# Rotary embedding and token-layout transposes inside the query/key/value projection, with its columns in the order value, key, query

## The reference

```python
q, k, v = jnp.split(xn @ w_qkv, 3, axis=-1)      # each (T, 1024): 8 heads x 2 maps x 64
q = rope(q, pos); k = rope(k, pos)               # x1*cos - x2*sin, x2*cos + x1*sin, halves of 64
# prompt: softmax over q k of both maps, a = p0 - lam * p1, o = a v; sample: the same over paged keys + new keys
return y, k, v                                   # rotated k rows and v rows are outputs too
```

## Time and profile before

| | us |
|---|---|
| median of three runs | 1459.0 |
| the profiled execution | 1462.04 |
| its span | 1460.7 |
| last scaling of the projection starts | 836.55 |
| first score matmul of the attention starts | 877.95 |

### The profile page before, as it was taken

One profiled execution on the slowest core, in us unless ns is written; L12 is line 12 of the kernel. 1 busy time (PEld: TensorE's weight loads), 2 busy tenths in 40 slices (PEclk: granted clock), 3 DMA queues, 4 the chain that ended last, 5 costly groups with the idle time before them and its releaser, 6 DMA issues.

```text
span 1460.7 us, 20977 instructions
## 1 busy us (share of the span) xinstructions
PE 1286.9 (88%) x8470; PEld 797.5 (55%) x8470; DVE 587.6 (40%) x1164; ACT 408.0 (28%) x717; POOL 146.9 (10%) x189
## 2 busy tenths in 40 slices
PE   6799999989879799999989959976987979999995
PEld 5676688866657543333347636654665755333332
DVE  3555367655333521212154574415533351221212
ACT  3443322254332211111153304434433221111112
POOL 5100031110002010101010060000000201110100
PEclk9899997799989799999999989978998979999998
DMA  8474354358638069999945737301873814999993
GB/s 239 143 211 125 114 161 124 100 174 288 236 126 340 22 257 421 420 421 421 422 155 158 241 101 259 117 1 58 291 248 129 337 41 191 421 422 420 421 421 118
DMA packets 112822, 340.16 MB, mean 233 GB/s; under 512 B 7486, under 2 KB 75402, under 8 KB 84048
## 3 DMA queue, kind: packets, MB, share of 16 engines
q1 hardware_dynamic: 107296, 322.20, 58.8%
q0 software_dynamic: 4992, 15.47, 3.4%
q10 hardware_dynamic: 432, 1.11, 0.2%
HBM read 328.21 MB, written 10.54 MB: 232 GB/s over the span
## 4 chain that ended last, share of the span: by engine, by line
PE 65%; DMA 17%; DVE 9%; issue 5%; ACT 3%; SPq 1%; POOL 1%; POOLq 0%; ACTq 0%; DVEq 0%
DMA arena<-in_w_exp_up 14%; PE ps L1961 10%; PE ps L547 8%; PE ps L549 8%; PE ps L548 8%; PE ps L2025 2%; PE ps L1440 2%; PE ps L1496 2%; PE ps L1415 2%; PE ps L2005 2%; PE ps L1480 2%; PE ps L1401 2%; DMA stg<-in_w_mem_k 1%; DVE wl L541 1%; PE ps L1428 1%
## 5 line engine op out<-in xcount | busy, mean ns | idle before, releaser
L1961 PE MATMUL ps<-arena,mkv 128*64 128x512 f32 x1024 | 230.0, 601 | 27.3 <-DMA arena<-in_w_exp_up 21.8
L547 PE MATMUL ps<-bx,wh 128*128 128x320 f16 (+1 forms) x640 | 194.5, 304 | 41.0 <-DVE bx L772 15.5
L548 PE MATMUL ps<-bx,wh 128*128 128x320 f16 (+1 forms) x640 | 194.3, 304 | 0.0
L549 PE MATMUL ps<-bx,wl 128*128 128x320 f16 (+1 forms) x640 | 194.1, 303 | 0.0
L541 DVE SCALAR_TENSOR_TENSOR wl<-stg,wh 128x1024 f16<-128x1024 f32 x128 | 157.8, 1272 | 87.4 <-ACT wh L534 86.5
L534 ACT ACTIVATE wh<-stg 128x1024 f16<-128x1024 f32 x128 | 128.4, 1049 | 216.8 <-PE ps L549 193.6
L1961 PEld LDWEIGHTS ps<-arena,mkv 128*64 128x64 f32 x1024 | 82.1, 138 | 170.7 <-issue 164.9
L2117 DVE TENSOR_TENSOR arena<-ps,arena 128x512 f16<-128x512 f32 x64 | 44.1, 688 | 143.2 <-ACT arena L2084 92.4
L547 PEld LDWEIGHTS ps<-bx,wh 128*128 128x128 f16 x640 | 65.0, 102 | 66.9 <-issue 34.7
L547 PE MATMUL ps<-arena,wh 128*128 128x320 f16 x288 | 88.4, 307 | 3.7 <-DVE arena L1363 3.0
L2121 DVE COPY arena<-ps 128x1 f32<-128x1 f32 x32 | 5.1, 158 | 211.6 <-PE ps L1983 211.6
(11 more groups left out here) (412 smaller groups left out, 1867.0 us busy)
## 6 DMA issues: line engine op xcount, KB each, us to landing
arena<-in_w_exp_gate SPq DMA_DIRECT2D x64, 1024.0 KB, 15.1
arena<-in_w_exp_up SPq DMA_DIRECT2D x64, 1024.0 KB, 17.2
arena<-in_w_exp_down SPq DMA_DIRECT2D x32, 1024.0 KB, 17.7
stg<-in_w_exp_down SPq DMA_DIRECT2D x32, 1024.0 KB, 17.5
arena<-in_cache_mem_k SPq DMA_DIRECT2D x16, 1024.0 KB, 6.9
arena<-in_cache_mem_v SPq DMA_DIRECT2D x16, 1024.0 KB, 5.2
stg<-in_w_in_a SPq DMA_DIRECT2D x28, 512.0 KB, 4.8
stg<-in_w_qkv_c SPq DMA_DIRECT2D x20, 512.0 KB, 4.6
```

Of the source, the lines that this page charges most:

```text
L547: nc.tensor.matmul(out, wh[:, s, at:at + 128], hi, start=start, stop=False)
L548: nc.tensor.matmul(out, wh[:, s, at:at + 128], lo, start=False, stop=False)
L549: return nc.tensor.matmul(out, wl[:, s, at:at + 128], hi, start=False, stop=stop)
L1961: last = nc.tensor.matmul(ps[64 * j:64 * j + 64, UB, :], xe[:, q % 2, j, k, :], gu[:, g % 2, j, :, k, :], start=(k == 0), stop=(k == KD - ...
```

## The change

The weight columns are streamed in the order value, key, query (the places in `zc` stay). The loops of the projection are written out per engine. Turns of the value come behind chunks 2 to 5, turns of the key behind chunks 8 to 11, evacuated by ScalarE ahead of its next split. The rotation of chunk i - 1 comes behind chunk i, from chunk 5 on, and that of the last behind the end. Sine products go to `xn` instead of `rstd`. Lambda is computed in the first two steps.

```diff
+              "qkv_v": lambda j: cols(a["w_qkv_c"][0], j * 256 + 2048),
+              "qkv_k": lambda j: cols(a["w_qkv_c"][0], j * 256),
-              "qkv": lambda j: cols(a["w_qkv_c"][0], j * 256), "out_c": lambda j: cols(a["w_out_c"][0], j * 256),
+              "qkv": lambda j: cols(a["w_qkv_c"][0], j * 256 - 2048), "out_c": lambda j: cols(a["w_out_c"][0], j * 256),
...
             if name == "qkv":
-                start = 1
+                load_units(name, 1, 2, MATRIX["qkv_v"])
+                load_units(name, 2, 4, MATRIX["qkv_k"])
+                start = 4
...
             V.tensor_copy(kT[:, :, 256:T], zc[:, 8:16, NP:T]).then_inc(S["bq_ready"], 1)
+            split_lo(dve, QKV + 13, 1)
         turned(0, 1)
...
-    def rope_pe(pe):
-        pe.wait_ge(S["w_ev"], UNIT["out_c"][0])
...
-    def rope_pool(pool, link):
...
-    def rope_dve(dve, link):
...
+    def qkv_chunk(i):
+        return (16, 18, 20, 22, 8, 10, 12, 14, 0, 2, 4, 6)[i]
+
+    QKV = UNIT["qkv"][0]
+    TURNS = {2: (0, 1), 3: (2,), 4: (3, 4), 5: (5,), 8: (6, 7), 9: (8,), 10: (9, 10), 11: (11,)}
+    TURN_BANK = (7, 4)
+    ROT_BANK = (5, 6)
+    rsin = xn[:, 0:2, :]
+
+    def turn_of(g):
+        src, dst = (16, vtok3) if g < 6 else (8, ktok3)
+        half, tile = g % 6 // 3, g % 3
+        t0, n = TILES[tile]
+        return (src + 4 * half, t0, n,
+                dst[0:n, tile, 512 * half:512 * half + 512].rearrange("p (a b) -> p a b", a=4))
+
+    def qkv_pe(pe):
+
+        def rotate(i):
+            pe.wait_ge(S["w_ev"], QKV + i + 1)
+            for c in range(2):
+                n = 2 * (i - 4) + c
+                if n >= 2:
+                    pe.wait_ge(S["rot_done"], n - 1)
+                nc.tensor.matmul(ps[:, ROT_BANK[c], 0:T], const("rot"), zc[:, qkv_chunk(i) + c, :], start=True,
+                                 stop=True).then_inc(S["rot_ps"], 1)
+
+        base = IN["qkv"][0]
+        pe.wait_ge(S["w_ev"], QKV)
+        for p in range(4):
+            if p % 2 == 0:
+                pe.wait_ge(S["w_lo"], QKV * 2 + p // 2 + 1)
+            pe.wait_ge(S["in_lo"], base + p + 1)
+            last = unit_mm(0, T, xh, xl, ks=(2 * p, 2 * p + 1))
+        last.then_inc(S["w_used"], 1)
+        sum_pe(pe, 3)
+        for i in range(1, 12):
+            pe.wait_ge(S["w_lo"], (QKV + i) * 2 + 2)
+            pe.wait_ge(S["w_ev"], QKV + i - 1)
+            unit_mm(i % 2, T, xh, xl).then_inc(S["w_used"], 1)
+            for g in TURNS.get(i, ()):
+                chunk, t0, n, _ = turn_of(g)
+                if g < 6:
+                    pe.wait_ge(S["w_ev"], QKV + (2 if g < 3 else 4))
+                else:
+                    pe.wait_ge(S["rot_done"], 4 if g < 9 else 8)
+                tr_pe(pe, G_DA + g, [zc[:, chunk + j, t0:t0 + n] for j in range(4)], 128, TURN_BANK[g % 2], 2)
+            if i >= 5:
+                rotate(i - 1)
+        rotate(11)
+
+    def qkv_act(act):
+        for i in range(12):
+            act.wait_ge(S["w_used"], QKV + i + 1)
+            if i == 2:
+                act.wait_ge(S["padded"], 1)
+            for g in TURNS.get(i, ()):
+                _, _, n, dst = turn_of(g)
+                act.wait_ge(S["tr_ps"], G_DA + g + 1)
+                nc.scalar.copy(dst, ps[0:n, TURN_BANK[g % 2], :].rearrange("p (a b) -> p a b", a=4)
+                               ).then_inc(S["tr_ev"], 1)
+            split_hi(act, QKV + i + 2, i % 2)
+            if i == 0:
+                norm_root_act(act, 3)
+                act.wait_ge(S["gneg_ready"], 2)
+                nc.scalar.activation(lams[:, 2:4], lams[:, 0:2], ACT.Exp).then_inc(S["gln_ready"], 1)
+
+    def qkv_pool(pool):
+
+        def cosines(i):
+            for c in range(2):
+                n, at = 2 * (i - 4) + c, qkv_chunk(i) + c
+                pool.wait_ge(S["rot_ps"], n + 1)
+                nc.gpsimd.tensor_tensor(zc[:, at, :], zc[:, at, :], const("cos"), ALU.mult).then_inc(S["rot_cos"], 1)
+
+        for i in range(4, 8):
+            cosines(i)
+        pool.wait_ge(S["tr_ev"], G_DA + 6)
+        nc.gpsimd.memset(zv_dead[:, 0:2048], 0.0)
+        for i in range(8, 11):
+            cosines(i)
+        pool.wait_ge(S["w_used"], QKV + 12)
+        nc.gpsimd.memset(pb[:, T:384], 0.0).then_inc(S["padded"], 1)
+        nc.gpsimd.memset(qd, 0.0).then_inc(S["padded"], 1)
+        cosines(11)
+
+    def qkv_dve(dve, link):
+        V = nc.vector
+        r = rstd[:, 1, :].unsqueeze(1).to_broadcast([128, 2, T])
+        lam_init = 0.8 - 0.6 * math.exp(-0.3)
+
+        def scale(i):
+            s, at = i % 2, qkv_chunk(i)
+            V.scalar_tensor_tensor(zc[:, at:at + 2, :], ps[:, 2 * s:2 * s + 2, 0:T], 1 / WSCALE, r, ALU.mult,
+                                   ALU.mult).then_inc(S["w_ev"], 1)
+
+        def rope(i):
+            for c in range(2):
+                dve.wait_ge(S["rot_ps"], 2 * (i - 4) + c + 1)
+                last = V.tensor_tensor(rsin[:, c, :], ps[:, ROT_BANK[c], 0:T], const("sin"), ALU.mult)
+            link(last)
+            for c in range(2):
+                n, at = 2 * (i - 4) + c, qkv_chunk(i) + c
+                dve.wait_ge(S["rot_cos"], n + 1)
+                V.tensor_tensor(zc[:, at, :], zc[:, at, :], rsin[:, c, :], ALU.add).then_inc(S["rot_done"], 1)
+
+        for i in range(12):
+            dve.wait_ge(S["w_used"], QKV + i + 1)
+            if i == 0:
+                split_lo(dve, QKV + 2, 0)
+                lv = lamv.rearrange("p (a d) -> p a d", a=4)
+                lp = rsin[:, 0, 0:128].rearrange("p (a d) -> p a d", a=2)
+                link(V.tensor_tensor(lp, lv[:, 0::2, :], lv[:, 1::2, :], ALU.mult))
+                V.reduce_sum(lams[:, 0:2], lp, AX.X).then_inc(S["gneg_ready"], 1)
+                dve.wait_ge(S["std_ready"], 2 * 3 + 2)
+                scale(0)
+                continue
+            scale(i)
+            if i < 11:
+                split_lo(dve, QKV + i + 2, i % 2)
+            if i == 1:
+                dve.wait_ge(S["gln_ready"], 2)
+                link(V.tensor_tensor(lams[:, 4:5], lams[:, 3:4], lams[:, 2:3], ALU.subtract))
+                link(V.tensor_scalar(lams[:, 4:5], lams[:, 4:5], -(1.0 + lam_init), None, ALU.add))
+                for col, name in ((5, "map_pair"), (6, "map_heads")):
+                    link(V.tensor_scalar(lams[:, col:col + 1], const(name), lams[:, 4:5], 1.0, ALU.mult, ALU.add))
+            if i >= 5:
+                rope(i - 1)
+        rope(11)
         dve.wait_ge(S["rot_done"], 16)
...
-        fused_pe(pe, "qkv", 3, (xh, xl))
-        rope_pe(pe)
+        qkv_pe(pe)
...
-        gemm_split_act(act, "qkv", 3)
-        act.wait_ge(S["gneg_ready"], 2)
-        nc.scalar.activation(lams[:, 2:4], lams[:, 0:2], ACT.Exp).then_inc(S["gln_ready"], 1)
+        qkv_act(act)
...
-        gemm_scale_dve(dve, "qkv", 3, zc[:])
-        rope_dve(dve, link)
+        qkv_dve(dve, link)
...
-        pool.wait_ge(S["w_ev"], UNIT["out_c"][0])
-        nc.gpsimd.memset(pb[:, T:384], 0.0).then_inc(S["padded"], 1)
-        rope_pool(pool, link)
+        qkv_pool(pool)
         pool.wait_ge(S["tr_ev"], G_Y)
...
-        nc.gpsimd.memset(zv_dead[:, 0:2048], 0.0)
-        nc.gpsimd.memset(qd, 0.0).then_inc(S["padded"], 1)
```

More of the change, by code:

```diff
@@ L437, in load_down, with load_units @@
                 sp.dma_start(dws[g % 2][:, j], w_down_f[2 * g + j]).then_inc(dw_in[g % 2], 16)
-        def load_units(name, start, stop):
+        def load_units(name, start, stop, matrix=None):
             u0 = UNIT[name][0]
+            matrix = MATRIX[name] if matrix is None else matrix
             with sp.Fori(start, stop) as i:
                 for s in range(2):
-                    load(i * 2 + (u0 + s), s, stage8(s), MATRIX[name](i * 2 + s))
+                    load(i * 2 + (u0 + s), s, stage8(s), matrix(i * 2 + s))
         def load_cache(kind, b, cache, dst, arrived):
@@ L522, in _ @@
                     for s in range(2):
-                        load(UNIT["qkv"][0] + s, s, early8(s), MATRIX["qkv"](s))
+                        load(UNIT["qkv"][0] + s, s, early8(s), MATRIX["qkv_v"](s))
                     sp.wait_ge(dw_used, NPAIR)
@@ L1686, in rope_pool @@
-    def rope_pool(pool, link):
[L1687 to L1690, removed]
-    def rope_dve(dve, link):
[L1693 to L1700, removed]
-        dve.wait_ge(S["rot_done"], 16)
[L1702 to L1708, removed]
-        link(nc.vector.tensor_scalar(lams[:, 4:5], lams[:, 4:5], -(1.0 + lam_init), None, ALU.add))
-        for col, name in ((5, "map_pair"), (6, "map_heads")):
-            link(nc.vector.tensor_scalar(lams[:, col:col + 1], const(name), lams[:, 4:5], 1.0, ALU.mult, ALU.add))
-        g = G_DA
-        for dst in (ktok3, vtok3):
-            for i, (t0, n) in enumerate(TILES):
-                for half in range(2):
-                    tr_dve(dve, g, dst[0:n, i, 512 * half:512 * half + 512].rearrange("p (a b) -> p a b", a=4), n,
-                           128)
-                    g += 1
```

## The result

The changed kernel took 1439.93 us (median of four runs, 1434.74 to 1441.08), the kernel before beside it 1459.88: ratio 0.9857, 95% interval 0.9823 to 0.9892, some 20 us less. A later comparison gave 0.9888 (0.9829 to 0.9947). The prediction was -12.2 us, 1446.8 with a range from 1441: right in sign, too small in size, and just outside its range.

A forecast was written before the change was run, and what follows sets the result against it. TensorE bounds the projection, a chain on other engines the stretch behind it. Loop +13.5, tail -26.1 and late keys +0.4 sum to -12.2 us: 1446.8 us from a median of 1459.0, range 1441 to 1454.

The forecast's parts named there:

- The bound and what hides it: Projection loop: TensorE sets the pace; the other engines' moved work is hidden, with 1 to 3 us of cover a chunk.
- the rivals on contention: Projection loop: VectorE and GpSimd obstruct each other and set the pace, fully or in part; 1451 to 1459 us, chance 0.10.
- a falling clock there: Projection loop: TensorE's granted clock falls, each microsecond at the low level costing 0.5; up to 1466.8 us, chance 0.04.
- The clock would hardly change that: Attention: nothing in the sum; first batch perhaps 1.6 us quicker, most of it lost to missing keys of batch 2.
- Fourteen of the sixteen rotation matmuls: Projection loop: fourteen rotations before the last chunk's end, at 0.57 each, add 8.0 us on TensorE.
- The tail: From the last chunk's scaling to the first attention scores: one chain of 15.3 us against 41.4, saving 26.1 us.
- The cosine product: GpSimd's rotary product, taken at 1.12 us per block in the chain behind the last scaling.
- the low halves of chunk 13: Behind the last scaling: VectorE's split for the next projection's weights delays TensorE's fourth turn by 2.4 us.
- Keys land at 28.8, costs 0.4: Attention: keys of batch 2 land 28.8 us after the last scaling, wanted at 28.4, costing 0.4 us.
- The sign of being wrong that it had named: Attention: TensorE waiting over 1 us for the keys of batch 2 would show the forecast wrong.
- The rule of the Trainium skill: Output DMAs: GpSimd's issues wait for VectorE's SBUF copies, keys 2 land 2.0 us later; 1448.8 us, chance 0.16.
- The whole: Whole kernel: loop, tail and late keys sum to -12.2 us, giving 1446.8 us.

The follow-up runs named there:

- double_cos: Changed kernel with every GpSimd cosine product of chunks 4 to 9 done twice, first into an unused place; 1449.03 us, one run.
- late_split: Changed kernel with the low halves of chunk 13 moved behind VectorE's first two evacuations of cached keys; 1438.97 us, ratio 0.9894 to the kernel before.
- early_out: late_split, with GpSimd starting the output DMAs of the value rows behind chunk 8 instead of at the end; 1440.65 us, ratio 0.9896.
- rotation_last: Changed kernel with value turns in the loop, but rotate(4) to rotate(11) and the key turns behind chunk 11; 1461.16 us, one run.
- late_split_keys: late_split, with the cached keys of batch 2 loaded before SP waits for the output DMAs; 1437.10 us, ratio 0.9858.
- turns_last: Changed kernel with all twelve turns behind chunk 11, still evacuated by ScalarE; 1443.47 us, one run.

## Why the prediction was right or wrong

- **The bound and what hides it: right.** TensorE paces the loop at the full clock (1.00), nothing in it waits (double_cos), and the rivals on contention and on a falling clock there did not occur.
- **"The clock would hardly change that": wrong, and it is the step that failed.** Its term in the sum was nothing. The prediction looked at the first batch alone and expected a gain there of up to 1.6 us; the granted clock there was 0.70 where it had been 0.86, which took 1.7. And it did not look behind the attention, where the clock rose from 0.66 to 0.78 in one profile and 0.69 in the other and gave 4.8 and 1.6 us. In the first profile no other term was off by as much.
- **"Fourteen of the sixteen rotation matmuls": miscounted.** Behind chunk i comes the rotation of chunk i - 1, so up to the last scaling there are twelve. The two of chunk 10 were counted here and again in the tail: 1.1 us. The sizes were a little high as well, another 1.2: rotations 0.535 and turns 0.43 instead of 0.57 and 0.50. Loop 11.2 instead of 13.5. (A chunk has 48 matmuls, not "48 matmul triples"; no term used that.)
- **The tail: right in its order, 14.3 instead of 15.3.** The cosine product was taken at 1.12, the pace of the rotary loop; between the projection's chunks it takes 0.84 to 0.87. In the rotary loop each product ran beside an add of VectorE; that this is what lengthened it was not tested. That the low halves of chunk 13 cost 2.4 of the tail late_split showed (2.3).
- **"Keys land at 28.8, costs 0.4": mechanism right, size wrong.** The values were asked for at 18.1 us as forecast, but TensorE had the keys at 30.3. The sign of being wrong that it had named, a wait of over 1 us for them, came: 1.19. In time it cost 0.9 beyond the clock's share; in other runs of the changed order the wait was up to 3.7 (early_out) and 9.7 (rotation_last).
- **The rule of the Trainium skill, "SBUF — State Buffer", section "SBUF: two separate sides", on a DMA issued from GpSimd: these runs do not bear it out.** In the changed kernel the four issues (849.87 to 852.44) lie beside VectorE's copies (850.71 to 852.99). The p_v rows took 8.3 us to land and the s_v rows 9.2, against 8.0 and 7.8 before; but in late_split, with the same copies beside the issues and the weight loads later, 8.0 and 8.1. So the copies cost little if anything; the earlier weight loads are the likelier reason for the rest, which no run isolates.
- **The whole.** With these sizes -12.2 becomes -18.2 in the first profile and -14.6 in the second (234.7 us from chunk 1 to the residual add, against 216.6 and 220.1). Without the stretch behind the attention it is -13.4 and -13.0: there the misses cancel, a loop and a tail cheaper by 3.3 and first batches dearer by some 2.2 to 2.6. That the prediction of the stage itself looks so close is in part luck.
- The rest up to the measured -20 (interval -16 to -26; by medians -18 in the later comparison) is within what executions of one kernel differ by ahead of the change: chunk 1 began anywhere from 762.2 to 775.3 us in the thirteen profiles.

Open: why just 45.8 us behind the attention in one profile of the changed kernel and 48.9 in the other, and anything from 45.4 to 50.5 in the edited ones. The pauses of TensorE inside the stretch are the same, and no run here fixes where the low stretches fall.

## What to carry to other kernels

Work of the other engines that follows a projection costs nothing when it is put between its chunks, as long as each engine's sum per chunk stays under TensorE's; count each moved instruction by its place against one fixed mark, so that none stands on both sides of it. When a pause goes, look at what was loaded during the pause, and at the order in which one queue asks for it. And look at the granted clock in the stages behind as well: in code that nobody touched it was 0.66 before, and 0.69 and 0.78 after. Before filling a pause to raise the clock, ask what the faster stage will wait for: here it was the DMA.

## What was not expected of the hardware

- GpSimd's product of 128x320 f32 took 0.84 to 0.87 us alone and 1.84 to 1.85 beside a VectorE split with two SBUF inputs, with nothing between in the loop. Two splits took 2.36 alone and 2.81 to 3.25 beside the products.
- 32 matmuls of constants ahead of the attention held the granted clock at 1.00 from the first scores to the maximum of batch 1 (0.86 in late_split_keys, the same kernel without them), and were worth 0.4 us before the first scores and 1.4 more up to that maximum; then the keys of batch 3 came too late.
- Chunk 1 of the projection began at 762 to 775 us, behind code of which the edits touch only the last few us, while from there to the last scaling nine profiles of the changed order (all but turns_last and rotation_last) agree within 0.01 us.
